# Two mixers of a hybrid encoder trunk: the recurrence chain put in the order of its operands, two pieces of it given to GpSimd, one more copy to ScalarE

## What is computed

```python
for l in range(DEPTH):
    mix = hybrid_mixer(x, ...)
    x = layer_norm(DEEPNORM_ALPHA * x + mix, ln1_g[l], ln1_b[l])
    ffn = swiglu(x, ...) if l % 2 == 0 else moe_swiglu(x, ...)
    x = layer_norm(DEEPNORM_ALPHA * x + ffn, ln2_g[l], ln2_b[l])
```

```python
r = sigmoid(uc @ wa + ba);  i = sigmoid(uc @ wx + bx)
log_a = -8 * r * softplus(-lam);  a = exp(log_a)
b = sqrt(-expm1(2 * log_a)) * (i * uf)          # uf is uc in float32
h = scan of h[t] = a[t] * h[t-1] + b[t]
y_lru = gelu(gate) * h
p = softmax over a band of 128 keys, with a sink;  y_attn = p @ v
mix = concatenate([y_lru, y_attn]) @ w_out
```

## Time and profile before

| | |
|---|---|
| median of 3 runs | 1028.14 us (1028.09 to 1028.23) |
| the profiled execution | 1028.07 us, of which the span is 1026.2 us |
| PE busy | 1004.6 us, 98% |
| DVE busy | 644.9 us, 63% |
| ACT busy | 538.8 us, 53% |
| POOL busy | 86.5 us, 8% |
| granted TensorE clock | 0.997 over the span |

### The profile page before, as it was taken

The page is one execution under the profiler, slowest core; times in us unless marked ns, Lnnn a source line. Parts: engine busy times, 40 slices in busy tenths (PEclk is TensorE's granted clock), DMA queues, the critical chain, the costliest instruction groups (busy, mean ns, idle before and its releaser), DMA issues.

```text
span 1026.2 us, 15030 instructions
## 1 busy us (share of the span) xinstructions
PE 1004.6 (98%) x5878; PEld 764.9 (75%) x5878; DVE 644.9 (63%) x885; ACT 538.8 (53%) x822; POOL 86.5 (8%) x93
## 2 busy tenths in 40 slices
PE   8999999999999999999999999999999999999995
PEld 7977888888798887886567886558887556888552
DVE  6998554545679889981049993119986117997103
ACT  5786343444459677771147772128775116776112
POOL 0002000000100069910000000000000000000000
PEclk9999999999999999999999999999999999999998
DMA  9945555545584659999999999999999999999993
GB/s 370 381 163 209 176 190 179 201 170 202 217 338 146 233 189 352 368 338 402 421 420 421 422 420 421 421 421 420 422 421 421 421 420 421 420 422 422 421 420 140
DMA packets 48153, 343.23 MB, mean 334 GB/s; under 512 B 5376, under 2 KB 5504, under 8 KB 6864
## 3 DMA queue, kind: packets, MB, share of 16 engines
q1 hardware_dynamic: 46656, 336.09, 81.5%
q0 software_dynamic: 992, 5.56, 1.5%
q10 hardware_dynamic: 432, 0.59, 0.2%
HBM read 341.17 MB, written 1.05 MB: 333 GB/s over the span
## 4 chain that ended last, share of the span: by engine, by line
PE 88%; DVE 7%; ACT 3%; issue 1%; DMA 1%; POOL 0%; POOLq 0%; SPq 0%; DVEq 0%
PE bank L989 15%; PE bank L638 13%; PE bank L640 13%; PE bank L639 13%; PE bank L980 7%; PE bank L831 7%; PE bank L834 6%; PE bank L837 6%; DVE low L1867 2%; PE bank L852 1%; DVE low L1514 1%; PE bank L1071 1%; PE bank L622 1%; DMA raw<-W 1%; ACT scr L1280 1%
## 5 line engine op out<-in xcount | busy, mean ns | idle before, releaser
L1867 DVE TENSOR_TENSOR low<-raw,whi 128x1024 fp32r<-128x1024 f32 x246 | 290.6, 1235 | 21.6 <-ACT whi L1384 21.3
L1384 ACT ACTIVATE whi<-raw 128x1024 fp32r<-128x1024 f32 x246 | 242.2, 1051 | 0.3 <-PE bank L640 0.3
L989 PE MATMUL bank<-raw,xg 128*64 128x256 f32 x1312 | 150.1, 380 | 0.0
L1514 DVE TENSOR_TENSOR low<-raw,whi 128x1024 fp32r<-128x1024 f32 x110 | 131.4, 1224 | 25.8 <-ACT whi L1168 24.8
L638 PE MATMUL bank<-whi,xgh 128*128 128x512 f32 x352 | 141.7, 402 | 0.0
L1921 DVE TENSOR_TENSOR he<-he,bank 128x128 f32<-128x128 f32 x44 | 12.7, 289 | 202.5 <-ACT he L1444 202.5
L640 PE MATMUL bank<-whi,xgl 128*128 128x512 f32 x352 | 137.7, 391 | 0.0
L639 PE MATMUL bank<-low,xgh 128*128 128x512 f32 x332 | 129.3, 390 | 0.0
L1168 ACT ACTIVATE whi<-raw 128x1024 fp32r<-128x1024 f32 x114 | 115.8, 1058 | 25.3 <-PE bank L640 17.4
L989 PEld LDWEIGHTS bank<-raw,xg 128*64 128x64 f32 x1312 | 92.1, 137 | 43.2 <-issue 2.4
L638 PE MATMUL bank<-whi,ah 128*128 128x512 f32 (+1 forms) x240 | 92.2, 384 | 4.1 <-DVE al L1526 2.0
(11 more groups left out here) (311 smaller groups left out, 1375.2 us busy)
## 6 DMA issues: line engine op xcount, KB each, us to landing
raw<-W SPq DMA_DIRECT2D x303, 1024.0 KB, 16.1
spare<-W SPq DMA_DIRECT2D x15, 1024.0 KB, 17.4
scr<-gb_d POOLq DMA_DIRECT2D x3, 1024.0 KB, 5.1
x<-x_d SPq DMA_DIRECT2D x2, 512.0 KB, 5.8
raw<-W SPq DMA_DIRECT2D x2, 512.0 KB, 6.1
scr<-wbd_d POOLq DMA_DIRECT2D x2, 512.0 KB, 9.1
spare<-gb_d POOLq DMA_DIRECT2D x1, 1024.0 KB, 9.8
out_d<-acc ACTq DMA_DIRECT2D x2, 256.0 KB, 2.5
```

Source lines behind the costliest of these rows:

```text
L989: last = nc.tensor.matmul(bank[n * NARROW:(n + 1) * NARROW, c % 2, 0:FC].rearrange("p (a n) -> p a n", a=2), xg[:, kk, at:at + NARROW], gu ...
L1384: nc.scalar.activation(whi[:, q % SPLIT, h * HW:(h + 1) * HW], piece_slot(home(J, i)[0])[:, h * HW:(h + 1) * HW], ACT.Copy).then_inc(hi_rd ...
L1514: V.tensor_tensor(low_of(p)[:, h * HW:(h + 1) * HW], piece_slot(place(p)[0])[:, h * HW:(h + 1) * HW], whi[:, p % SPLIT, h * HW:(h + 1) * H ...
L1867: V.tensor_tensor(low_slot(s)[:, h * HW:(h + 1) * HW], piece_slot(s)[:, h * HW:(h + 1) * HW], whi[:, q % SPLIT, h * HW:(h + 1) * HW].bitca ...
```

## The change

It does five things in both mixers:

1. The product of input gate and `uc` (L1675) leaves DVE for POOL, which waits for the sigmoids and then does all 1024 columns at once, and DVE waits for it (`gated_u`) ahead of `inputs`.
2. The low part of the first half of piece `p0+8` leaves DVE for POOL too (`low_half`, semaphore `half_lo`); PE waits on that.
3. On DVE both groups under the root come right behind the low halves of `p0+7`; the cast and the low part of the first half of y_lru come ahead of scans 2 and 3; `low_y(1)` goes from behind the first group of score maxima to behind the second.
4. On ACT the high part of piece `p0+8` goes ahead of the copy of y_lru's second half.
5. The copy of the third of four probability groups goes from DVE to ACT.

```diff
+POOL_HALVES = (8, MIXP + FFP + 8)
...
+            def low_half(p):
+                pool.wait_ge(hi_rdy, 2 * p + 1)
+                nc.gpsimd.tensor_tensor(low_of(p)[:, 0:HW], piece_slot(place(p)[0])[:, 0:HW],
+                                        whi[:, p % SPLIT, 0:HW].bitcast(F32), ALU.subtract).then_inc(half_lo, 1)
...
                 pool.dma_start(scr[:, 0:1024], wbd_d[l]).then_inc(wbd_in, 16)
+                pool.wait_ge(uc_rdy, CT * (l + 1))
+                pool.wait_ge(sig_rdy, 4 * (l + 1))
+                nc.gpsimd.tensor_tensor(ri[:, 1], ri[:, 1], uc[:], ALU.mult).then_inc(gated_u, 1)
+                low_half(POOL_HALVES[l])
...
+                elif h == 0 and p in POOL_HALVES:
+                    pe.wait_ge(half_lo, POOL_HALVES.index(p) + 1)
...
-                            pe.wait_ge(pt2_sb if t else pt_sb, 2 * l + 2)
+                            pe.wait_ge(pt_sb, 3 * l + 2 + t)
+                            if t:
+                                pe.wait_ge(pt2_sb, l + 1)
...
+                hi(p0 + 8)
                 act.wait_ge(ylru_rdy, 2 * l + 2)
                 nc.scalar.activation(xTh[:, 2:4, :], tmp[:, 2:4, :], ACT.Copy).then_inc(yh_rdy, 1)
-                hi(p0 + 8)
...
-                for b in range(2):
+                for b in range(3):
                     act.wait_ge(pt_ps, 4 * l + b + 1)
...
-                dve.wait_ge(sig_rdy, 4 * (l + 1))
-                link(V.tensor_tensor(ri[:, 1], ri[:, 1], uc[:], ALU.mult))
...
+                    dve.wait_ge(gated_u, l + 1)
                     dve.wait_ge(sq_rdy, 2 * l + g + 1)
...
+                under_root(0)
+                under_root(1)
                 inputs(0)
                 scan(0)
                 scan(1)
                 inputs(1)
                 gated(0)
-                scan(2)
-                scan(3)
                 dve.wait_ge(ylru_rdy, 2 * l + 1)
                 dve.wait_ge(used, 2 * (p0 + 7))
                 link(V.tensor_copy(xTh[:, 0:2, :], tmp[:, 0:2, :]))
                 low_y(0)
+                scan(2)
+                scan(3)
                 gated(1)
                 for b in range(4):
-                    if b == 1:
+                    if b == 2:
                         low_y(1)
-                        lo_half(p0 + 8, 0)
...
-                for b in range(2, 4):
-                    dve.wait_ge(pt_ps, 4 * l + b + 1)
-                    V.tensor_copy(pt[:, b], bank[:, SB[b], :].rearrange("p (r q) -> p r q", r=4)).then_inc(pt2_sb, 1)
+                dve.wait_ge(pt_ps, 4 * l + 4)
+                V.tensor_copy(pt[:, 3], bank[:, SB[3], :].rearrange("p (r q) -> p r q", r=4)).then_inc(pt2_sb, 1)
```

More of the change, by code:

```diff
@@ L335, in build @@
         at_rdy = sem("at_rdy")
+        sq_rdy = sem("sq_rdy")
         v_rdy = sem("v_rdy")
-        sq_rdy = sem("sq_rdy")
+        gated_u = sem("input_gate_times_u_rdy")
+        half_lo = sem("second_down_piece_low_half_rdy")
         ylru_rdy = sem("ylru_rdy")
@@ L1515, in lo_half @@
                                 whi[:, p % SPLIT, h * HW:(h + 1) * HW].bitcast(F32),
-                                ALU.subtract).then_inc(lo_rdy, 3 if after_pool else 1)
+                                ALU.subtract).then_inc(lo_rdy, 3 if after_pool else 2 if p in POOL_HALVES else 1)
             def lo(p):
@@ L1673, in mixer, with under_root @@
                 lo(p0 + 7)
-                dve.wait_ge(sig_rdy, 4 * (l + 1))
-                link(V.tensor_tensor(ri[:, 1], ri[:, 1], uc[:], ALU.mult))
-                for g in range(2):
+                def under_root(g):
                     h = slice(2 * g, 2 * g + 2)
```

## The result

| | median | range, executions | ratio to before |
|---|---|---|---|
| before | 1028.09 us | 1027.85 to 1028.76, 20 | |
| changed | 1029.72 us | 1029.46 to 1032.08, 20 | 1.0017, 95% interval 1.0011 to 1.0023 |

The account below looks back on a forecast made before the run. PE was taken to bound the kernel (88% of the chain), waiting in the mixers on DVE and ACT. L804 at +1.87 - 0.60 = +1.27 us per mixer, twice 2.54, on 1028.07 gave 1030.6 us; range 1027.0 to 1032.2.

Parts of the forecast that it names:

- forecast mechanism: Both mixers: each long POOL instruction holds DVE's SBUF instructions until it ends; 1029.9 to 1031.4 us, chance 0.50.
- a port only partly held: Rival: POOL holds the port, but not against copies or not against tiny instructions; 1028.5 to 1029.6 us, chance 0.24.
- Step 1: Gate product on POOL: DVE's 256-column copy starts 2.33 us later, 1.26 is given back, the root is ready 1.07 later.
- Step 2: ACT's row up to the dummy exponential, and the scores on PE, each come 1.07 us later.
- Step 3: DVE's new order: `gated(0)` to `gated(1)` takes 3.07 us in place of 2.84; reordering gains nothing there.
- Step 4: Low half on POOL to 62.4: DVE's four-column L1729 waits 1.95 us for it.
- Steps 5 and 6: ACT's exponentials begin at 62.55, +2.0 us, without the 0.29 stall; DVE's normalising begins at 67.25, 1.87 later.
- Steps 7 and 8: One DVE copy less gives back 0.60 us; L804, the product with v, starts at 72.47, +1.27, PE's transposes hidden.
- The rival in which tiny instructions pass: Copies wait for POOL but the four-column L1729 does not: +0.65 us per mixer, 1029.4; within a chance of 0.24.
- copies pass: DVE's copies are not held by POOL's product, its low half is: +0.37 us per mixer, 1028.8; within a chance of 0.24.
- No contention: First rival: POOL holds nothing, L804 comes 1.2 us earlier in mixer 0, 1.0 in mixer 1; 1025.9 us, chance 0.18.
- POOL's late turn: Rival: POOL is held throughout by DVE, costing some 2 us more per mixer; 1033 us or so, chance 0.06.

Follow-up runs that it names:

- e1: Changed kernel with the gate product back on DVE ahead of the roots, the low half still on POOL: 1027.92 us, ratio 0.9997.
- e2: Changed kernel with the low half of the second output piece back on DVE, the product still on POOL: 1028.93 us, ratio 1.0016.
- e6: Kernel before plus a POOL memset of 1024 columns in mixer 0, on which nothing in the chain depends: 1029.37 us, ratio 1.0012.
- e5: Kernel before plus a POOL product of uc with itself (1024 columns) in mixer 0, on which nothing in the chain depends: 1030.53 us, ratio 1.0022.
- e7: Changed kernel with POOL's product started only when DVE's copies of v are done: 1031.24 us, ratio 1.0027.
- e10: Kernel before plus the extra POOL product in mixer 0 and six filler products on PE before each mixer's scores: 1029.59 us, ratio 1.0014.

## Why the prediction was right, step by step

The time forecast was 1030.6, measured 1029.72: 1.63 us lost where 2.5 were forecast. The mechanism was the one forecast. Its first size was too large, and that put the forecast on the other side of the 0.2% line: I gave slower 0.44 and within 0.40, and it came to lie just within. By the number alone the case is not decided: 1029.72 lies 0.18 below the range that I gave the forecast mechanism (1029.9 to 1031.4) and 0.12 above that of a port only partly held (1028.5 to 1029.6). What decides is the rows of steps 1 and 4, which show both holds, and `e1` and `e2`, which take them away one by one.

- **Step 1**, the product holds DVE's copies: right, mis-sized. The copy lost 2.09 us (2.38 for 0.29), not 2.33. I had POOL wait for the running copy to end at 44.64; it ran its 2.42 us from 44.38 at once, and DVE's copies that it met, from 44.04, still took their 0.49. The root was ready at 51.88 + 0.69 = 52.57, 0.72 late against 51.85 and not 1.07. About 0.1 of that is no effect of the change: this execution stood 0.1 us ahead at the copies (44.04 for 44.15).
- **Step 2**, ACT and the scores 1.07 late: 0.73 (the second root at 52.61 for 51.88), by the same error.
- **Step 3**, the new order costs 0.23 on DVE: right. From `gated(0)` to `gated(1)` it takes 58.38 - 55.28 = 3.10 us (forecast 3.07, before 2.84).
- **Step 4**, the four-column bias waits for POOL's low half: right. It took 1.94 where 0.16 stood, so it waited 1.78; the forecast had 1.95 of waiting. The rival in which tiny instructions pass is out.
- **Steps 5 and 6**: exponentials at 62.12 (forecast 62.55), no stall at the second group, normalising at 66.79 (forecast 67.25), 1.41 late and not 1.87. Of the difference of 0.46, 0.35 is step 1's.
- **Steps 7 and 8**: L820 at 72.10 waiting for DVE's single copy, forecast 72.47. The copy taken off DVE gave back 0.51 (1.41 less 0.90) and not 0.60. Per mixer 0.90 and 1.03, not 1.27. PE's transposes ended 0.9 late and were hidden, as said.
- **The rivals.** That copies pass was weighed at 1028.8: the copy rows refute it, and `e6` shows a copy held even by a write. In between lay the one in which only the bias passes, 1029.4, nearest to the time of all: the bias row refutes it. No contention (1025.9) falls in `e5`. POOL's late turn did not occur; in `e7` POOL waited for one subtraction and no more.
- **What the prediction did not have** is the clock. PE's wait before the scores grew by 0.7 us. In the profiled execution, with 1.81 us of waiting, the clock stayed at 1.00; behind the longer waits of `e5`, `e6` and `e7` it fell. A loss of DVE time there can cost more than itself.
- **Where the gain was**: in the order of the chain, only not in POOL. Product behind the roots on DVE and the copies on ACT come near what the first rival forecast for a change without contention (1025.9 forecast, 1026.40 and 1026.01 measured), by another way than that rival's.

## What to carry to other kernels

Work moved to GpSimd is free for VectorE only where VectorE meanwhile runs instructions that it does not hold; here that was a maximum that reads PSUM. Otherwise count the whole GpSimd time (2.4 us for 1024 columns) against the 1.1 to 1.3 us that VectorE saves, and look at which instruction it will land on, since a bias of four columns on the critical path waits as long as a long one would. First put the work of the busy engine behind what another engine waits for: the same product cost 0.83 us less in the shadow of ScalarE's roots. And treat a growing wait of TensorE as a price of its own, since the clock behind it may fall: fillers in that wait won 0.94 us back (`e10` against `e5`).

## What the runs showed of the hardware

- A POOL product of 1024 columns with two different operands took 2.40 to 2.42 us, the same with one tensor read twice 1.90, a memset 0.95.
- A one-input DVE copy from SBUF to SBUF was held by POOL's product (2.38 and 1.87 for 0.29) and by its memset (1.34 for 0.49 in the pair). A two-input instruction of four columns was held by the low half (1.94 for 0.16). Two-input subtractions were held by the product (4.56 for 2.36) and not by the memset (2.36). The Trainium skill, "SBUF — State Buffer", section "Who interferes with whom", states that a two-input instruction contends with a GpSimd instruction that reads SBUF and not with one that only writes, and that one in a two-port mode, which a copy can enter, contends with GpSimd. The runs agree; no row names the mode of a copy, but the one of 256 columns took 0.29 us where L1882, with two inputs of 256, one of them in PSUM, took 0.41.
- DVE reading PSUM was not held: the maximum of the scores (L1744 in the changed kernel) took 0.69 us with POOL's low half beside it.
- With PE waiting 1.92, 2.02 and 2.65 us before the scores the granted clock behind the wait fell to 0.50 to 0.61 (`e6`, `e7`, `e5`); with 1.81 it was 1.00 in two profiled executions (the changed kernel and `e2`), whose kernels have single executions 2.4 and 3.5 us above their medians, with a mean clock of 0.993.
